# The down-projection of a two-layer trunk, done as seven block products, with sums made by negated copies and accumulating DMAs

## The chip, the core and the metric

One core of one Trainium2 chip runs the whole program. TensorE (PE in the profile) multiplies, VectorE (DVE), ScalarE (ACT) and GpSimd (POOL) do the rest, SyncE (SP) issues the DMAs. The metric is the device time of one execution in microseconds; three runs of the kernel before gave 2281.78, 2283.82 and 2288.46 us.

## The reference

Two layers run over 1024 prompt tokens and 64 sample tokens (8 sequences of 8), width 1024, inner width 2816, in float32. The change lies in the last matrix product of each layer and in the norm behind it:

```python
up = jnp.einsum('btd,df->btf', x, w_up)
hp = jnp.concatenate([conv_prefix, up], axis=1)
hc = conv_b + sum(conv_w[i] * hp[:, i:i + T] for i in range(CONV_WIDTH))
g, u = hc[..., :D_FF], hc[..., D_FF:]
y = jnp.einsum('btf,fd->btd', jax.nn.gelu(g, approximate=False) * u, w_down)
x = layer_norm(DEEPNORM_ALPHA * x + y, ln2_g, ln2_b)
```

The `x` of the last line is itself a norm's output, with gain `ln1_g` and bias `ln1_b`.

## The kernel before

The tokens are nine tiles: 0 to 7 of 128 prompt tokens, 8 (`NB`) with the 64 sample tokens. Every float32 operand is split into a rounded copy (`..h`, written by ACT) and the remainder (`..l`, a subtraction on DVE or POOL), and a product is three matmuls: high by high, high by low, low by high. The engines run programs of their own, with the order of work written out by hand and semaphores between them; nothing is reordered at run time.

A layer has four stages. The input projection and the mixing heads come first, then the output projection and a norm, whose result without gain and bias is kept in DRAM (`z_scr`). The up-projection then runs over 22 blocks `f` of 128 channels (gate and up); it is already computed as seven half-size products (`times`), with POOL making the sums of the weight blocks (`sum_up`, `lo_up`) and DVE joining the products (`joined`: `c11`, `u2`, `v`, ...). For each block ACT moves the sample columns (`moves`) and writes the first filter term (`tap_gate` into `hg[f % 2]`, `tap_up`), DVE adds the other terms (`conv_gate`, `conv_up`), ACT applies GELU, DVE multiplies (`product`), and SP stores the block to `a_scr[f]` (`act_rows`), 552 KB.

The down-projection goes over three groups of three tiles, and in each over all 22 rows `k` of blocks of `w_down`: a unit `d` loads `w_down[128k : 128k+128, :]` (512 KB) and the three tiles' columns of `a_scr[k]` (192 KB), ACT and DVE split both (`down_hi`, `act_hi`, `down_lo`, `act_lo`), and PE issues six matmuls of 512 columns a tile, four for the sample tile. Four slots hold split weights, three hold split activations, and a slot is written when PE has left the unit that used it. When a group ends, DVE adds the residual from PSUM (`joined_rz`), takes the statistics (`moments`), and later applies mean, deviation, gain and bias to the tile (`gained`, two instructions of 1024 columns). The residual itself is prepared by POOL: `residual` multiplies the tile read back from `z_scr` by the gain row and adds the bias row, two instructions a tile:

```python
pool.tensor_tensor(rz, rz, gain[0][0:tokens(t), :], ALU.mult).then_inc(S["xp1"], 1)
pool.wait_ge(S["xp1"], l * NTOK + t + 1)
pool.tensor_tensor(rz, rz, gain[1][0:tokens(t), :], ALU.add).then_inc(S["xp"], 1)
```

PE transposes finished tiles for the next layer (`turn_x`) between units, six tiles inside the down-projection and three behind it, and the input projection of layer 1 works on chunks of 384, 384 and 320 tokens (`two_chunks`). SP's queue carries all DMAs, in order; POOL issues none.

## Time and profile before

| | |
|---|---|
| runs | 2281.78, 2283.82, 2288.46 us, median 2283.82 |
| the profiled execution, its span | 2283.5 us |
| up-projection of layer 0, window | 580 to 877.3 us and before |
| down-projection of layer 0 | 877.3 to 1145.8 us |
| down-projection of layer 1 | ends at 2266.8 us |
| DMA, mean over the span | 118 GB/s |

The span runs from the first to the last instruction. The profile counts an engine as busy while it computes; PE and PEld (its weight loads) overlap. PEclk is the granted clock of TensorE as a share of full speed.

### The profile page before, as it was taken

What the parts mean: (1) busy time and instruction counts of PE and PEld (TensorE: products, weight loads), DVE (VectorE), ACT (ScalarE), POOL (GpSimd) and SP (SyncE); (2) the same over time, 40 slices, a digit from 0 to 9 for tenths busy, and PEclk for the clock granted to TensorE, in tenths of its full rate; (3) what the DMA queues carried; (4) which work ended last, traced back from release to release, by engine and by line L of the source; (5) the groups of instructions that cost most, each with busy time, mean ns of one, the idle gap of its engine ahead of it and who ended that gap; (6) DMA issues with size and microseconds to landing.
All of it is one profiled execution on the core that took longest, in us unless ns stands there. A gap on an engine that the chain in (4) does not pass through costs nothing.

```text
span 2283.5 us, 35524 instructions
## 1 busy us (share of the span) xinstructions
PE 2185.3 (96%) x14132; PEld 1986.4 (87%) x14132; DVE 1651.1 (72%) x2004; ACT 981.5 (43%) x1767; POOL 832.3 (36%) x444
## 2 busy tenths in 40 slices
PE   7999999899999999999999999989999999999996
PEld 7997677799999998888899876779999999988885
DVE  1477767878788886787636687677777878867677
ACT  3226755544344434343422276464434443443342
POOL 1115255554554450320311242446455445311311
PEclk9999999999999999999999999999999999999998
DMA  6303166223322325665562122641332233365762
GB/s 157 86 20 84 33 206 175 65 58 86 88 69 77 86 69 203 235 213 195 193 140 48 48 51 87 179 152 51 83 86 77 69 88 86 98 250 185 241 217 92
DMA packets 208766, 269.74 MB, mean 118 GB/s; under 512 B 31953, under 2 KB 167377, under 8 KB 208529
## 3 DMA queue, kind: packets, MB, share of 16 engines
q1 hardware_dynamic: 208600, 267.46, 39.2%
q8 instruction: 113, 1.85, 0.3%
q14 instruction: 53, 0.43, 0.1%
HBM read 217.65 MB, written 46.13 MB: 116 GB/s over the span
## 4 chain that ended last, share of the span: by engine, by line
PE 76%; DVE 14%; ACT 5%; issue 3%; POOL 2%; DMA 0%; SPq 0%; ACTq 0%; DVEq 0%; POOLq 0%
PE ps L2153 37%; PE ps L1872 17%; PE ps L1831 9%; PE ps L2092 5%; DVE bnst L1292 1%; PE ps L1897 1%; DVE rl L1491 1%; PE ps L1976 1%; DVE rzc L1278 1%; PE ps L1955 1%; DVE cb L1564 1%; POOL bl L762 1%; PE ps L1991 1%; DVE Sb L1610 1%; PE ps L2002 1%
## 5 line engine op out<-in xcount | busy, mean ns | idle before, releaser
L2153 PE MATMUL ps<-bt,bh 128*128 128x272 f32 (+1 forms) x3520 | 591.1, 290 | 18.7 <-DVE bt L1397 9.3
L2153 PEld LDWEIGHTS ps<-bt,bh 128*128 128x128 f32 x3520 | 503.3, 190 | 20.3 <-DVE bt L1397 9.7
L979 ACT ACTIVATE bh<-wblk 128x512 fp32r<-128x512 f32 x308 | 183.6, 624 | 483.1 <-POOL wblk L774 268.2
L2153 PE MATMUL ps<-bt,bl 128*128 128x272 f32 (+1 forms) x1760 | 369.1, 290 | 0.0
L2153 PEld LDWEIGHTS ps<-bt,bl 128*128 128x128 f32 x1760 | 278.4, 190 | 0.0
L762 POOL TENSOR_TENSOR bl<-wblk,bh 128x512 fp32r<-128x512 f32 x98 | 168.4, 1721 | 283.8 <-ACT bh L979 283.8
L1872 PE MATMUL ps<-rh,ah 128*128 128x512 f32 x792 | 245.6, 391 | 4.6 <-DVE ah L1502 3.2
L1872 PE MATMUL ps<-rl,ah 128*128 128x512 f32 x792 | 244.1, 389 | 0.0
L2153 PE MATMUL ps<-ba,bh 128*128 128x272 f32 (+2 forms) x1408 | 233.8, 288 | 4.0 <-DVE gu L1438 2.4
L1415 DVE TENSOR_TENSOR bl<-wblk,bh 128x512 fp32r<-128x512 f32 x210 | 169.0, 837 | 91.7 <-ACT bh L979 91.7
L1491 DVE TENSOR_TENSOR rl<-wrow,rh 128x1024 fp32r<-128x1024 f32 x132 | 189.5, 1437 | 42.5 <-ACT rh L1035 42.3
L1872 PE MATMUL ps<-rh,al 128*128 128x512 f32 x704 | 216.8, 389 | 0.0
L2153 PEld LDWEIGHTS ps<-ba,bh 128*128 128x128 f32 x1408 | 199.2, 188 | 5.3 <-DVE gu L1438 2.8
L787 POOL TENSOR_TENSOR rzd<-rzd,gain 128x1024 f32<-128x1024 f32 (+1 forms) x18 | 49.8, 2764 | 416.5 <-DMA rzd<-z_scr 416.5
L1831 PE MATMUL ps<-xh,wh 128*128 128x384 f32 (+1 forms) x576 | 194.1, 337 | 0.9 <-POOL wl L732 0.9
L1831 PE MATMUL ps<-xh,wl 128*128 128x384 f32 (+1 forms) x576 | 189.9, 330 | 0.0
L1831 PE MATMUL ps<-xl,wh 128*128 128x384 f32 (+1 forms) x576 | 189.7, 329 | 0.0
L740 POOL TENSOR_TENSOR rl<-wrow,rh 128x1024 fp32r<-128x1024 f32 x48 | 118.4, 2473 | 175.0 <-ACT rh L872 141.4
L1872 PEld LDWEIGHTS ps<-rh,ah 128*128 128x128 f32 x792 | 147.0, 188 | 38.3 <-issue 9.2
L1872 PEld LDWEIGHTS ps<-rl,ah 128*128 128x128 f32 x792 | 148.7, 188 | 31.1
L1035 ACT ACTIVATE rh<-wrow 128x1024 fp32r<-128x1024 f32 x132 | 138.1, 1049 | 45.1 <-DMA wrow<-in_w_down 30.8
L1872 PEld LDWEIGHTS ps<-rh,al 128*128 128x128 f32 x704 | 132.2, 188 | 27.7
(222 smaller groups left out, 4042.3 us busy)
## 6 DMA issues: line engine op xcount, KB each, us to landing
wrow<-in_w_down SPq DMA_DIRECT2D x132, 512.0 KB, 4.8
wblk<-in_w_up SPq DMA_DIRECT2D x88, 512.0 KB, 5.3
a_scr<-hg SPq DMA_DIRECT2D x44, 552.0 KB, 3.5
araw<-a_scr SPq DMA_DIRECT2D x88, 192.0 KB, 4.4
wrow<-in_w_out SPq DMA_DIRECT2D x48, 256.0 KB, 5.1
wrow<-in_w_out SPq DMA_DIRECT2D x24, 512.0 KB, 4.2
wraw<-in_w_in SPq DMA_DIRECT2D x10, 1024.0 KB, 6.3
z_scr<-rzc SPq DMA_DIRECT2D x16, 512.0 KB, 4.6
```

Source lines behind the costliest of these rows:

```text
L740: pool.tensor_tensor(rl[c % 2][:], wrow[(c + 2) % 4][:], rh[c % 2][:].bitcast(F32), ALU.subtract).then_inc(S["w_lo"], 1)
L762: pool.tensor_tensor(bl[b][:], block_of(f, b), bh[b][:].bitcast(F32), ALU.subtract).then_inc(S["u_lop"], 1)
L787: pool.tensor_tensor(rz, rz, gain[0][0:tokens(t), :], ALU.mult).then_inc(S["xp1"], 1)
L979: act.activation(bh[b][:], block_of(f, b), ACT.Copy).then_inc(S["u_hi"], 1)
L1035: act.activation(rh[dn_slot(d)][:], wrow[(d + 2) % 4][:], ACT.Copy).then_inc(S["d_hi"], 1)
L1278: e = dve.scalar_tensor_tensor(out=r, in0=r, scalar=ALPHA, in1=ps[0:q, 2 * i:2 * i + 2, :], op0=ALU.mult, op1=ALU.add)
L1415: dve.tensor_tensor(bl[b][:], block_of(f, b), bh[b][:].bitcast(F32), ALU.subtract).then_inc(S["u_lov"], 1)
L1491: dve.tensor_tensor(rl[s][:], wrow[(d + 2) % 4][:], rh[s][:].bitcast(F32), ALU.subtract).then_inc(S["d_lo"], 1)
L1831: e = nc.tensor.matmul(out, lhs, rhs, start=(m == 0), stop=(m == n - 1))
L1872: e = nc.tensor.matmul(ps[:, 2 * i + half, :], lhs, rhs[:, 512 * half:512 * half + 512], start=(first and m == 0), stop=(final and m == le ...
L2092: e = nc.tensor.matmul(ps[:, 2 * i + n, :], m_tile(t, KORD[kk], low), right[:, 512 * n:512 * n + 512], start=start, stop=stop)
L2153: e = nc.tensor.matmul(up_half(f, b, n), lhs, rhs[:, c:HW_] if n else rhs[:, 0:c], start=(k == 0 and m == 0), stop=(k == HK - 1 and m == 2))
```

## The change

Two things keep their form: the split into high and low parts, and 128x512 results in PSUM. The down-projection is now one level of a seven-product scheme. Prompt tokens are halved (tiles 0 to 3, tiles 4 to 7), the inner rows are halved (even and odd blocks `f`), and the output columns are halved (0 to 511, 512 to 1023). Each of the seven products (`P_1`, `P_2`, `P_3`, `P_6`, `P_5`, `P_7`, `P_4`, in this order) has 11 steps `s`, in which four token tiles of one operand block meet one 128x512 piece of a weight block. The sample tokens aren't part of the scheme; their rows ride along in the four products whose right side is a plain block of `w_down`.

The sums that the scheme needs are made in three ways. On the activations: ACT writes a negated copy of half a block (`negated`), SP stores it to the new DRAM buffers `e_scr` and `f_scr` (`neg_out`), and POOL issues accumulating DMAs that add other half blocks on top (`act_add`, three for each pair of blocks), while the up-projection runs. On the weights: the four blocks are loaded once a layer and stay in SBUF; ACT writes a negated copy of a block (`weight_neg`), and an accumulating DMA from `w_down` adds a block to it (`weight_add`), so `T_1`, ..., `T_4` come one after the other. On the results: the first product is copied to `p1`, DVE adds or subtracts products from PSUM into the residual rows `rzd` (`join`, `second`), and four accumulating DMAs add `p1` to the residual rows (`residual_add`).

All nine residual tiles are in SBUF at once. ACT multiplies the two rows of the first norm by ALPHA (`scaled_gains`), and POOL still multiplies and adds them. The gain and the bias row of the second norm are now applied by POOL for tiles 0 to 3, 8 and 5 (`gained`), behind a normalising instruction on ACT (`normal2`), and by DVE for tiles 4, 6 and 7. The input projection of layer 1 takes chunks of 512, 288 and 288 tokens, and five tiles are transposed inside the down-projection. The core of the diff:

```diff
-CH = [(0, 384), (384, 768), (768, T)]
+CHS = [[(0, 384), (384, 768), (768, T)]] + [[(0, HT), (HT, 800), (800, T)]] * (DEPTH - 1)
...
+KP = FT // 2
+NP = 7
+NST = NP * KP
+P_1, P_2, P_3, P_6, P_5, P_7, P_4 = range(NP)
+PX, PY, PZ = [6, 7, 2, 5], [3, 4, 0, 1], [2, 5, 6, 7]
+P_BANKS = {P_1: PX, P_2: PY, P_3: PX, P_6: PY, P_5: PX, P_7: PY, P_4: PZ}
+P_SAMP = {P_1: PY[3], P_2: PX[0], P_3: PY[0], P_5: PY[0]}
+BY_POOL = [0, 1, 2, 3, 8, 5]
+BY_DVE = [4, 6, 7]
+KGRP = [(0, 4), (4, 8), (8, KP)]
+X_AT = {62: 0, 64: 1, 68: 2, 70: 3, 72: 8}
...
+            def neg_out(l, k, which):
+                sp.wait_ge(S["neg"], neg_a(l, k, which) + 1)
+                if which == 0:
+                    sp.dma_start(e_scr[k, :, 0:3:2, :], hx[:, 0:1, :].to_broadcast([P, 2, HT])).then_inc(S["e_out"], 16)
+                else:
+                    sp.dma_start(f_scr[k], hx[:, 1, :]).then_inc(S["f_out"], 16)
...
+                sp.wait_ge(S["u_p"], 7 * (l + 1) * FT)
+                down_block(l, "w11", 2, 4, 7)
+                down_block(l, "w11", 3, 7, KP)
+                for s in range(4, NST):
+                    if s == 4:
+                        gains(l, 0)
+                        gains(l, 1)
+                        z_back(l, NB)
+                    elif s in (5, 7):
+                        z_back(l, s - 5)
+                        z_back(l, s - 4)
+                    elif s == 6:
+                        sample_raw(l, 2)
+                        down_block(l, "w21", 0, 0, 6)
+                    elif s == 8:
+                        down_block(l, "w21", 1, 6, KP)
+                    elif s == 9:
+                        act_rows(l, FT - 1)
...
+                    elif s == 17:
+                        down_block(l, "w22", 0, 0, KP)
+                    elif s == 18:
                         conv_rows(l, NRB - 1)
...
+                    act_block(l, s)
...
+            def act_add(l, k, i):
+                n = l * KP + k
+                if i == 0:
+                    pool.wait_ge(S["e_out"], 16 * (n + 1))
+                    pool.dma_start(e_scr[k, :, 0:3:2, :], hg[0][:, HT:2 * HT].unsqueeze(1).to_broadcast([P, 2, HT]),
+                                   accum_op=ALU.add).then_inc(S["adds0"], 16)
+                elif i == 1:
+                    pool.wait_ge(S["prod"], l * FT + 2 * k + 2)
+                    pool.wait_ge(S["a_out0"], 32 * (n + 1))
+                    pool.wait_ge(S["adds0"], 16 * (n + 1))
+                    pool.dma_start(e_scr[k, :, 1:3, :], hg[1][:, HT:2 * HT].unsqueeze(1).to_broadcast([P, 2, HT]),
+                                   accum_op=ALU.add).then_inc(S["adds1"], 16)
+                else:
+                    pool.wait_ge(S["f_out"], 16 * (n + 1))
+                    pool.wait_ge(S["adds1"], 16 * (n + 1))
+                    pool.dma_start(f_scr[k], e_scr[k, :, 2, :], accum_op=ALU.add).then_inc(S["adds2"], 16)
...
+            def weight_add(l, which, g):
+                k0, k1 = KGRP[g]
+                tile, block, c = {T_1: (w11, 0, HT), T_2: (w22, 1, HT), T_3: (w12, 0, HT), T_4: (w21, 1, 0)}[which]
+                pool.wait_ge(S["neg"], neg_t(l, which, g) + 1)
+                after(pool, f"wadd{g}", 16 * (4 * l + which))
+                src = w_down[l].rearrange("(k two p) n -> two p k n", two=2, p=P)[block][:, k0:k1, c:c + HT]
+                pool.dma_start(tile[:, k0:k1, :], src, accum_op=ALU.add).then_inc(S[f"wadd{g}"], 16)
...
+            def gained(l, t):
+                n, q = l * len(BY_POOL) + BY_POOL.index(t), tokens(t)
+                rz = rzd[t][0:q, :]
+                if t == 0:
+                    pool.wait_ge(S["gain_landed"], 64 * (l + 1))
+                pool.wait_ge(S["ln_z"], z2_n(l, t) + 1)
+                pool.tensor_tensor(rz, rz, gain[2][0:q, :], ALU.mult).then_inc(S["n_ym"], 1)
+                pool.wait_ge(S["n_ym"], n + 1)
+                pool.tensor_tensor(rz, rz, gain[3][0:q, :], ALU.add).then_inc(S["n_yp"], 1)
...
                 for f in range(1, FT):
                     lo_up(l, f, B_11)
                     lo_up(l, f, B_12)
-                    for b in SUMS:
+                    for b in SUMS[:3]:
                         sum_up(l, f, b)
+                    sum_up(l, f, B_S3)
+                    if f >= 5 and f % 2:
+                        act_add(l, (f - 5) // 2, 2)
+                    if f >= 3 and f % 2:
+                        act_add(l, (f - 3) // 2, 0)
+                    elif f >= 4:
+                        act_add(l, (f - 4) // 2, 1)
+                act_add(l, KP - 2, 1)
+                residual(l, NB)
+                act_add(l, KP - 2, 2)
+                act_add(l, KP - 1, 0)
+                weight_add(l, T_1, 0)
+                for t in range(4):
                     residual(l, t)
+                act_add(l, KP - 1, 1)
+                weight_add(l, T_1, 1)
+                act_add(l, KP - 1, 2)
+                weight_add(l, T_1, 2)
+                residual_add(l, R_P1)
+                for t in range(4, NB):
+                    residual(l, t)
+                for which in (T_2, T_3, T_4):
+                    for g in range(len(KGRP)):
+                        weight_add(l, which, g)
+                for which in (R_U2T, R_U2B, R_U2C):
+                    residual_add(l, which)
+                for t in TOP:
+                    gained(l, t)
...
                 if f >= 2:
-                    act.wait_ge(S[f"a_out{f % 2}"], 16 * (l * (FT // 2) + f // 2))
+                    if f % 2:
+                        act.wait_ge(S["a_out1"], 16 * (l * KP + f // 2))
+                        act.wait_ge(S["adds1"], 16 * (l * KP + f // 2))
+                    else:
+                        act.wait_ge(S["a_out0"], 32 * (l * KP + f // 2))
+                        act.wait_ge(S["adds0"], 16 * (l * KP + f // 2))
                 act.activation(hg[f % 2][:], gu[f % 2][:, 0, C0:C0 + CV], ACT.Identity, scale=par[:, f, 16:17], bias=par[:, f, 19:20])\
...
+            def negated(l, k, which):
+                act.wait_ge(S["prod"], l * FT + 2 * k + which + 1)
+                after(act, ("adds0", "f_out")[which], 16 * (l * KP + k))
+                act.activation(hx[:, which, :], hg[which][:, 0:HT], ACT.Copy, scale=-1.0).then_inc(S["neg"], 1)
...
+                for s in range(NST):
+                    if s + 2 < NST:
+                        down_hi(l, s + 2)
+                        act_hi(l, s + 2)
...
+                    elif 58 <= s < 63:
+                        if s < 62:
+                            deviation2(l, TOP[s - 58])
+                        if s == 61:
+                            deviation2(l, NB)
+                        normal2(l, TOP[s - 58])
...
+                for s in range(NST):
+                    if s + 2 < NST:
+                        down_lo(l, s + 2)
+                        act_lo(l, s + 2)
...
+                    elif s in (57, 58):
+                        for i in range(2):
+                            stats(l, 2 * (s - 57) + i, 1)
+                            moments2(l, 2 * (s - 57) + i)
+                        if s == 58:
+                            scaled2(l, 0)
+                    elif s == 59:
+                        stats(l, NB, 1)
+                        moments2(l, NB)
+                        scaled2(l, 1)
+                    elif s in (60, 61):
+                        scaled2(l, s - 58)
+                        for i in range(2):
+                            join(l, J_VB, 2 * (s - 60) + i)
...
+                    lh_, ll_, rh_, rl_ = ah[s % 3][:, P * i:P * i + P], al[s % 3][:, P * i:P * i + P], dh[s % 3][:], dl[s % 3][:]
+                    for m, (lhs, rhs) in enumerate(((lh_, rh_), (lh_, rl_), (ll_, rh_))):
+                        e = nc.tensor.matmul(ps[:, P_BANKS[p][i], :], lhs, rhs, start=(fresh and m == 0), stop=(final and m == 2))
...
+                for s in range(2, NST - 3):
+                    down_ready(s)
+                    down_step(s)
+                    if s == 4:
+                        rows_turn(NRB - 1)
+                    if l < DEPTH - 1 and s in X_AT:
+                        turn_x(l + 1, X_AT[s])
+                for tiles in ((0, 1), (2, 3)):
+                    for s in range(NST - 3, NST):
+                        down_ready(s)
+                        down_step(s, tiles)
```

## Rows read from the trace of the kernel before

**Rows 1.** the page, part 1: busy time, share of the span, instructions:

```profile
span 2283.5 us, 35524 instructions
...
PE 2185.3 (96%) x14132; PEld 1986.4 (87%) x14132; DVE 1651.1 (72%) x2004; ACT 981.5 (43%) x1767; POOL 832.3 (36%) x444
...
```

**Rows 2.** engine busy by window: layer 0, up-projection, then down-projection:

```profile
...
core 0: us, PE busy (x) PEld busy (x) DVE busy (x) ACT busy (x) POOL busy (x), PEclk, DMA share, GB/s
580.00:877.30 297.30, 297.30 (x2376) 297.30 (x2375) 237.70 (x258) 124.40 (x211) 137.83 (x79) 1.00 0.29 83
877.30:1145.80 268.50, 266.61 (x1197) 219.39 (x1196) 196.94 (x213) 109.01 (x173) 54.40 (x20) 1.00 0.62 208
...
```

**Rows 3.** timeline of PE, start of the down-projection of layer 0:

```profile
...
877.33 0.62 PE L1872 MATMUL ps<-rh,ah 128*128 128x512 f32 x2
...
889.14 0.39 PE L1872 MATMUL ps<-rh,al 128*128 128x512 f32 x1
```

**Rows 4.** groups by line and form, DVE: count, busy us, mean ns, idle before:

```profile
...
L1491 DVE TENSOR_TENSOR rl<-wrow,rh 128x1024 fp32r<-128x1024 f32 x132 | 189.5, 1437 | 42.5 <-ACT rh L1035 42.3
L1415 DVE TENSOR_TENSOR bl<-wblk,bh 128x512 fp32r<-128x512 f32 x210 | 169.0, 837 | 91.7 <-ACT bh L979 91.7
...
L1292 DVE BATCH_NORM_STATS2 bnst<-rzd 128x6 f32<-128x512 f32 x32 | 20.6, 685 | 0.4
...
```

**Rows 5.** timeline, both engines, while POOL prepares tiles 0 to 2:

```profile
...
917.84 1.23 DVE L1491 TENSOR_TENSOR rl<-wrow,rh 128x1024 fp32r<-128x1024 f32 x1 [1.24 <-ACT rh L1035]
...
921.67 3.42 DVE L1491 TENSOR_TENSOR rl<-wrow,rh 128x1024 fp32r<-128x1024 f32 x1
...
923.96 3.38 POOL L787 TENSOR_TENSOR rzd<-rzd,gain 128x1024 f32<-128x1024 f32 x1
...
925.01 2.75 DVE L1498 TENSOR_TENSOR al<-araw,ah 128x384 fp32r<-128x384 f32 x1
...
929.97 3.39 POOL L787 TENSOR_TENSOR rzd<-rzd,gain 128x1024 f32<-128x1024 f32 x1
...
```

**Rows 6.** ACT instructions by line, two answers: min/median/max ns, first and last start:

```profile
...
L905 ACT ACTIVATE rzc<-rzc,nmr,rst x18: 1231/1247/1252, 325.7 to 1525.5; 128x1024 f32<-128x1024 f32 x16, 64x1024 f32<-64x1024 f32 x2
...
L979 ACT ACTIVATE bh<-wblk x308: 612/620/638, 394.2 to 1982.6; 128x512 fp32r<-128x512 f32 x154
...
```

**Rows 7.** timeline of one block of the up-projection, all engines:

```profile
...
705.93 0.64 ACT L979 ACTIVATE bh<-wblk 128x512 fp32r<-128x512 f32 x1 [3.37 <-PE ps L2153]
...
707.83 1.28 POOL L781 TENSOR_TENSOR wblk<-wblk,wblk 128x512 f32<-128x512 f32 x1 [4.14 <-DVE bl L1415]
...
711.01 1.31 ACT L1011 ACTIVATE hg<-gu,par 128x1104 f32<-128x1104 f32 x1
...
719.68 0.71 DVE L1429 TENSOR_TENSOR gu<-gu,ps 128x544 f32<-128x544 f32 x1
...
728.47 1.28 POOL L781 TENSOR_TENSOR wblk<-wblk,wblk 128x512 f32<-128x512 f32 x1 [3.81 <-DVE bl L1415]
...
```

**Rows 8.** DMA issues: KB each, median us to landing:

```profile
...
a_scr<-hg SPq DMA_DIRECT2D x44, 552.0 KB, 3.5
...
gain<-in_ln_b SPq DMA_DIRECT2D x4, 512.0 KB, 8.9
...
```

**Rows 9.** one window of 5 us in the down-projection:

```profile
...
910.00:915.00 5.00, 5.00 (x24) 4.14 (x23) 2.39 (x4) 2.54 (x3) 0.00 (x0) 1.00 1.04 408
...
```

**Rows 10.** timeline of ACT and DVE around the start of the down-projection:

```profile
...
880.74 1.29 ACT L1018 ACTIVATE hu<-gu,par 128x1104 f32<-128x1104 f32 x1
...
884.58 1.36 DVE L1449 SCALAR_TENSOR_TENSOR hg<-gu,par,hg 128x1104 f32<-128x1104 f32 x1
...
```

**Rows 11.** timeline, end of the kernel:

```profile
...
2266.41 0.61 PE L1872 MATMUL ps<-rl,ah 128*128 128x512 f32 x2
...
2278.60 1.28 DVE L1316 SCALAR_TENSOR_TENSOR rzd<-rzd,rst,gain 64x1024 f32<-64x1024 f32 x1
```

**Rows 12.** waits of PE at the layer boundary (us, times, longest):

```profile
...
PE ps L1850 <- DVE xl L1259: 1.6, 1, 1.6
...
```

More of the change, by code:

```diff
@@ L364, in m_part, with half_of @@
+        def half_of(t, half):
+            return rzd[t][0:tokens(t), HT * half:HT * half + HT]
         def m_part(op, low):
@@ new lines, in scaled_gains, with first_out, deviation2 @@
+            def scaled_gains(l):
+                act.wait_ge(S["gain_landed"], 64 * l + 32)
+                for n in range(2):
+                    act.activation(gain[n][:], gain[n][:], ACT.Copy, scale=ALPHA).then_inc(S["gain_ok"], 1)
+            def first_out(l):
+                for i in range(4):
+                    act.wait_ge(S["d_tile"], 4 * (l * NP + P_1) + i + 1)
+                    act.activation(p1[:, i, :], ps[:, PX[i], :], ACT.Copy).then_inc(S["p1_ev"], 1)
+            def deviation2(l, t):
+                q = tokens(t)
+                act.wait_ge(S["ln_ag"], ln2_n(l, t) + 1)
+                act.activation(rst2[0:q, t, :], mv2[0:q, t, 1:2], ACT.Sqrt, bias=epsT[0:q, 0:1]).then_inc(S["ln_sd"], 1)
@@ L1073, in body @@
                 else:
-                    for t in G3[2]:
+                    for t in range(4, NB):
                         x_hi(l, t)
@@ new lines, in second, with stats @@
+            def second(l, i):
+                dve.wait_ge(S["d_tile"], 4 * (l * NP + P_6) + i + 1)
+                dve.wait_ge(S["radd"], 16 * (RADDS * l + R_P1))
+                dve.tensor_tensor(p1[:, i, :], p1[:, i, :], ps[:, PY[i], :], ALU.add).then_inc(S["joins"], 1)
+            def stats(l, t, half):
+                q = tokens(t)
+                if t == NB:
+                    dve.wait_ge(S["joins"], JOINS * l + (J_S5 if half else J_S2) + 2)
+                else:
+                    j = (J_VT if half else J_C11) if t < 4 else J_C22 if half else J_C21
+                    dve.wait_ge(S["joins"], JOINS * l + j + t % 4 + 1)
+                dve.bn_stats(out=bst[0:q, t, 6 * half:6 * half + 6], in_=half_of(t, half)).then_inc(S["ln_bn"], 1)
@@ new lines, in body @@
+                    if l < DEPTH - 1 and s in X_AT:
+                        x_lo(l + 1, X_AT[s])
+                for t in (4, 5):
+                    join(l, J_C21, t - 4)
+                    stats(l, t, 0)
+                    moments2(l, t)
+                scaled2(l, 4)
+                scaled2(l, 5)
+                dve.wait_ge(S["gain_landed"], 64 * (l + 1))
+                gained(l, 4)
+                for t in (6, 7):
+                    join(l, J_C21, t - 4)
+                    stats(l, t, 0)
+                    moments2(l, t)
@@ L1818, in body @@
+                scaled2(l, 6)
+                gained(l, 6)
+                scaled2(l, 7)
+                gained(l, 7)
                 if l < DEPTH - 1:
-                    for t in G3[2]:
+                    for t in range(4, NB):
                         x_lo(l + 1, t)
@@ L1864, in turn_z @@
                 for k in range(KD):
-                    e = pe.transpose(ps[:, z_bank(t) + k // 4, P * (k % 4):P * (k % 4) + q], rzc[slot_of(0, t)][0:q, P * k:P * k + P], ident[0:q, 0:q])
+                    e = pe.transpose(ps[:, z_bank(t) + k // 4, P * (k % 4):P * (k % 4) + q], rzc[slot_of(t)][0:q, P * k:P * k + P], ident[0:q, 0:q])
                 e.then_inc(S["z_tr"], 1)
-            def six(i, pairs, first, final):
-                for m, (lhs, rhs) in enumerate(pairs):
-                    for half in range(2):
-                        e = nc.tensor.matmul(ps[:, 2 * i + half, :], lhs, rhs[:, 512 * half:512 * half + 512],
-                                             start=(first and m == 0), stop=(final and m == len(pairs) - 1))
-                return e
             pe.wait_ge(S["id_landed"], 16)
@@ new lines, in down_step @@
+                def down_step(s, tiles=(0, 1, 2, 3)):
+                    p, k = divmod(s, KP)
+                    if p in P_SAMP and k == KP - 1:
+                        down_samples(s)
+                    for i in tiles:
+                        down_tile(s, i)
+                    if p in P_SAMP and k < KP - 1 and 3 in tiles:
+                        down_samples(s)
+                down_ready(0)
+                down_step(0, (0, 1))
+                down_ready(1)
+                down_step(1, (0, 1))
```

822 lines of the change are left out of this document (525 added, 297 removed), and 2 rows, old and new, of the table S.

## The prediction, made before the changed kernel ran

> **What bounds the kernel now.** I read the page's first part, then the windows, then timelines inside the windows. TensorE (PE) is busy 2185.3 of 2283.5 us [rows 1]. The two windows of layer 0 show it busy without a gap through the up-projection and 266.6 of 268.5 us through the down-projection, at a granted clock of 1.00, its upper level of 2.4 GHz [rows 2]. So in these stages the time is the number of matmuls by the time of each. In the down-projection 52 matmuls of 512 columns start between 877.33 and 889.14 us, 0.227 us each [rows 3]. The windows give DVE as busy 196.9 us of that window, ACT 109.0, POOL 54.4, the DMA engines 0.62 [rows 2]: there is room, if nothing has to wait in the wrong place.
>
> **What it removes.** Per layer the old down-projection issues 22 x (8 x 6 + 4) = 1144 matmuls. The new one issues 7 products x 11 steps x 4 tiles x 3 = 924, and 4 x 11 x 2 = 88 for the sample rows: 1012. The shape stays 128x128 by 512 columns. 132 fewer x 2 layers x 0.227 us = **-59.9 us**. A step is now 12 matmuls, 2.72 us, or 14, 3.18 us, where the sample rows ride along (first, second, third and fifth product). PE transposes the same nine tiles between layers. The input projection of layer 1 has the same matmuls over 512 + 288 + 288 instead of 384 + 384 + 320 columns, 1088 both ways: nothing.
>
> **Work per step, and lead.** A step needs two ACT copies of 128x512 at 0.62 us [rows 6] and two DVE subtractions of 128x512, 0.62 (half of the 1.23 us that 1024 columns take when POOL is idle [rows 5]) to 0.84 us, the mean with POOL beside them [rows 4]. That is 1.3 us on each engine against 2.72 us. The joins (42 a layer) and statistics (18) of 512 columns cost DVE about 0.7 us each [rows 4], 42 us in 225. All hidden by mean load. With three operand slots DVE ends step s about 1.9 us after PE ends step s-3, so PE has a lead of 2 x 3.18 - 1.9 = 4.4 us (3.5 us at 2.72): any delay beyond that is lost.
>
> **POOL beside DVE.** Here is the change's first price. While POOL multiplies and adds the residual's gain and bias rows, DVE and POOL take turns: POOL ran 3.38 and 3.39 us, DVE's two subtractions took 3.42 and 2.75 us, of which the first takes 1.23 alone and the second, with 384 columns, less, and two POOL instructions with two of DVE took 929.97 - 923.96 = 6.0 us [rows 5]. With the new 512-column pairs (0.6 + 0.6 instead of 1.23 and about 0.5) I take 5.5 us a pair. Before, a unit of 18 matmuls (4.1 us) needed such a pair and three such units passed under PE's lead; now a step of 3.18 us needs one. The Trainium skill ("SBUF — State Buffer", Who interferes with whom) says that a DVE instruction with two SBUF inputs contends with a GpSimd instruction that reads SBUF and that one waits out the other; the trace agrees, and by that rule the joins, which read PSUM, go free.
>
> *Residual rows.* Tiles 0 to 3, then 4 to 7: eight POOL instructions in a row each, four pairs, 22 us against 12.7 us of PE, 9.3 late, less the lead of 4.4: 5 us. Two stretches, two layers: **+20 us**. Lower bound 0 (if POOL's DMA waits space them out), upper 9.3 x 4 = 37.
>
> *Gain and bias rows after the norm*, moved from DVE (five tiles) to POOL, steps 58 to 62. Here ACT and DVE also go in lockstep: ACT issues the normalising instruction of a tile (1.25 us [rows 6]) only after DVE's `scaled2`, DVE does that after the subtractions of step s+2, and ACT's copies for s+3 are queued behind it. In a round, counted from the end of a normalising instruction: POOL starts its two instructions, ACT copies, DVE's two subtractions are done after 6.2 us, scalar work 0.35 (1.2 in the first, with statistics), ACT 1.25: 7.8 to 8.7 us. From the start of PE's step 58: first tile normalised at 5.3; operands of step 61 at 11.5, of 62 at 20.2, 63 at 28.0, 64 at 35.8, 65 at 41.0. Undisturbed, 65 would start at 7 x 2.72 = 19.0. So **+22 us a layer, +44**. Lower bound: POOL alone sets the pace, 27 us for ten instructions against 13.6, less the lead, 10 a layer; and 0 if DVE slips between.
>
> **Start of the stage.** Step 2's operands come after ACT's `tap_up`, which ended 4.7 us after the stage's start at 882.0 [rows 10], a new negation (0.62) and two copies (1.24): DVE at 884.5, PE wants it at 883.7. Then DVE's two gate instructions (2.75, two like the 884.58 row), GELU (1.2, a little under the 1.31 of `tap_gate` [rows 7]), the copies (1.24) and the last subtraction of step 3: 890.3, 2.6 late; then two more filter instructions and sample rows: 1.7 late. 5.1 us, less the old stage's own 0.9 in this place: **+8.5 us**. DMA: about 9.5 MB must land before step 8's operands, SP's queue being in order; at 408 GB/s [rows 9] that is 23 us against the 25 of eight steps, so I add nothing; at the 286 GB/s of the up-projection (83 / 0.29 [rows 2]) it would be 33, +8 a layer. The two later bursts (4.5 MB around step 17) stand behind four slots of prefetch.
>
> **Accumulating DMAs in the up-projection.** The trace of before has none, and no DMA from POOL. `tap_gate` of block f now waits for an addition out of the buffer it overwrites, and POOL issues that only after the last block sum of f+1. In the trace that sum ends at 709.1 and `tap_gate` starts at 711.0; what hangs on it (gate filter, `c11`, up filter, `u2`) ends at 720.4 [rows 7]. PE ended the product that reuses `u2`'s banks at 705.9 and so starts the next, 24 matmuls of 0.125 us [rows 2], at 705.9 + 20.6 - 3.0 = 723.5. Slack 3.1; the DMA may take 1.9 + 3.1 = 5.0 us, and each us more is a us per block. The plain store of the same buffer lands in 3.5 us [rows 8]; an accumulation reads its target too, 0.52 MB, 1.3 us at 408 GB/s; 0.3 for POOL: 5.1, the edge. In every second block another DMA stands ahead of it: 0.34 us to issue and 0.26 MB twice over, +1.0 to 1.6. I take +1.0 us in ten blocks a layer: **+20 us**. Bounds: 0 (3.5 us as the store), and 8.9, the slowest landing [rows 8]: 3.9 and 4.9 us, 84 a layer. The Trainium skill ("DMA: Bandwidth & Descriptors", Specifications) gives about 1 us to the first byte from GpSimd against about 0.6 from the hardware path; no run here shows it. By it the sum would be 0.1 us larger per block, some 4 us.
>
> The later accumulations (weights, 1 MB, needed five to seven steps on, 14 us or more; the residual, 9 steps on) would have to take three times a plain load to be felt: nothing.
>
> **Ends.** At the layer boundary tiles 4 to 6 must be split before the second chunk, and DVE splits them after its last gained tile, 11 us after the last matmul; the first chunk covers 10.9 us. I take +2 us on the old 1.6 [rows 12]: **+2**. End of the kernel: from the last matmul (2266.8) to DVE's last (2279.9) 13.1 us [rows 11], then 3.6 for the store. Now two half tiles remain at the last matmul: join, statistics, two gained tiles, 11.4 us: **-1.7**.
>
> **Sum.** -59.9 + 20 + 44 + 8.5 + 20 + 2 - 1.7 = +32.9. The profiled run is 2283.5 us, the median of the runs 2283.8, so they may be compared: 2283.5 + 32.9 = **2316 us**. By itself the down-projection comes out about even: 30 us less work a layer, 36 us of waits.
>
> **Rivals.**
> 1. *The shared port does not reach PE.* If DVE's instructions slip between POOL's, or the lockstep does not form, the 64 us go: 2252 us. For it: in the old stage PE lost 1.9 us in all beside the same overlap [rows 2, 5]. Against: step and lead are shorter. It decides from about half: with 40 of the 64 us gone the kernel is faster. Chance 0.26.
> 2. *The accumulations are slow.* At 6.7 us instead of 5.1, 1.7 and 2.7 us a block, 42 a layer, 33 more than the ten of the forecast: 2316 + 66 = 2382 us; at 8.9, 2464. For: the target is read and written in memory. Against: the DMA engines are 0.29 busy there [rows 2]. Chance 0.22.
> 3. *Bytes bound the start.* 8 us a layer more: 2332 us, within the forecast's own range. Chance 0.10.
> 4. Forecast: 0.42, own range 2295 to 2340.
>
> Less than 0.3% (7 us) I can't tell from no change. Faster: rival 1 and little more, 0.27. Same: the crossing between rival 1 and the forecast, 0.08. Slower 0.65. The range goes from 2242 (rival 1 with half of the 20 us of the DMAs gone) to 2400 (rival 2).
>
> **What would show it.** 1012 matmuls of 512 columns a layer at 0.227 us. DVE's `dl` and `al` subtractions with maxima near 3.3 us where POOL works on `rzd`; PE waiting for DVE `al` in steps 61 to 65 for about 5 us each. In the up-projection, idle time of ACT before L1011's successor released by a DMA, and blocks of alternating length, 20.7 and 21.7 us. The forecast is wrong if the window of the up-projection is unchanged, or longer by over 40 us, or if the 77 steps take less than 250 us.

## The result, and the profile after

The changed kernel takes 2564.6 us (median of 4 runs, 2562.4 to 2571.1) against 2283.2 us for the kernel before (4 runs): a ratio of 1.1227, 95% interval 1.1205 to 1.1248. It is 281 us slower, where 33 us were forecast; 2565 lies far outside the range of 2242 to 2400. The profiled run has a span of 2565.0 us.

Page of the changed kernel, parts 1, 3 and 4 (beside [rows 1]):

```profile
PE 2232.4 (87%) x13868; PEld 1997.6 (78%) x13868; DVE 1671.0 (65%) x2064; ACT 1044.6 (41%) x1867; POOL 994.7 (39%) x566
...
q1 hardware_dynamic: 222424, 261.69, 32.7%
q0 software_dynamic: 31008, 60.30, 14.7%
...
PE ps L2713 11%; DMA e_scr<-hg 10%; PE ps L2301 9%; DMA araw<-a_scr 4%; POOL wblk L969 3%; PE ps L2560 3%; POOL bl L961 3%; POOL wblk L973 3%; DVE al L1913 2%; POOL wblk L977 2%; DVE hg L1873 2%; DVE hg L1870 2%; POOL wblk L980 2%; DVE dl L
```

PE has fewer matmuls and yet is "busy" longer (2232 against 2185 us), and two DMAs stand in the chain that ended last: POOL's accumulation `e_scr<-hg` with 10%, the load `araw<-a_scr` with 4%. Windows of layer 0: the whole up-projection of the kernel before, then the up-projection and the down-projection of the changed kernel (the down-projection before is in [rows 2]):

```profile
396.40:877.30 480.90, 469.51 (x3726) 468.46 (x3727) 385.95 (x424) 207.83 (x350) 237.18 (x136) 0.99 0.28 79
```

```profile
399.30:984.10 584.80, 502.37 (x3726) 495.55 (x3727) 387.18 (x425) 215.91 (x370) 266.04 (x165) 0.93 0.42 106
984.10:1291.15 307.05, 257.44 (x1057) 205.73 (x1056) 199.48 (x245) 131.10 (x201) 101.85 (x50) 0.92 0.72 191
```

The up-projection, whose matmuls the change doesn't touch, grew by 103.9 us (480.9 to 584.8); the down-projection, with 11.5% fewer matmuls, by 38.5 (268.5 to 307.05). Layer 1 repeats it, with 578.8 and 305.2 us. Both windows also show a lower granted clock of TensorE, 0.93 and 0.92 instead of 0.99 and 1.00: PE stood idle again and again, and the same 3726 instructions of the up-projection count 502 us of busy time instead of 470. In the down-projection the matmuls are busy 257.4 us, where 266.6 less 30 would be 236.6: about 21 us of that stage went into slower matmuls, the rest of its loss into waiting. Waits of PE over the whole kernel (us in total, times, longest):

```profile
PE ps L2621 <- ACT gu L1276: 134.0, 40, 7.4
PE ps L2713 <- DVE al L1913: 96.5, 25, 9.3
```

**The up-projection.** Timeline of one even and the start of one odd block (start, us; in brackets the idle time before and what ended it):

```profile
718.54 1.29 POOL L980 TENSOR_TENSOR wblk<-wblk,wblk 128x512 f32<-128x512 f32 x1 [3.82 <-DVE bl L1836]
719.77 1.19 POOL L993 DMA_DIRECT2D e_scr<-hg  x1
...
725.56 1.31 ACT L1304 ACTIVATE hg<-gu,par 128x1104 f32<-128x1104 f32 x1 [3.87 <-DMA e_scr<-hg]
...
728.49 0.60 ACT L1276 ACTIVATE gu<-ps 128x544 f32<-128x544 f32 x1
729.15 0.77 PE L2621 MATMUL ps<-bt,bh 128*128 128x272 f32 x4 [1.58 <-ACT gu L1276]
...
743.19 1.29 POOL L980 TENSOR_TENSOR wblk<-wblk,wblk 128x512 f32<-128x512 f32 x1 [3.81 <-DVE bl L1836]
...
744.42 0.88 POOL L998 DMA_DIRECT2D f_scr<-e_scr  x1
...
745.01 1.55 POOL L987 DMA_DIRECT2D e_scr<-hg  x1
```

POOL ends its last block sum (L980) at 719.83 and issues the accumulation at once; `tap_gate` (L1304) starts only when that has landed, at 725.56, 5.7 us after the sum. In the odd block the smaller accumulation stands ahead in the queue, and `tap_gate` started at 753.13, 8.7 us after the sum. From L980 to L980 the block takes 24.65 us, the next one 28.2 (to 771.35); before, 20.6 [rows 7]. PE's wait is named after `snap` (L1276), which ACT does behind `tap_gate`, `tap_up` and the new negation. What hangs on `tap_gate` on DVE runs without a gap, up to the split (L1836) that POOL's next last sum waits for:

```profile
726.90 1.37 DVE L1870 SCALAR_TENSOR_TENSOR hg<-gu,par,hg 128x1104 f32<-128x1104 f32 x1 [5.08 <-ACT hg L1304]
...
735.79 2.43 DVE L1889 TENSOR_TENSOR hg<-hg,hu 128x1104 f32<-128x1104 f32 x1
...
738.15 2.38 DVE L1836 TENSOR_TENSOR bl<-wblk,bh 128x512 fp32r<-128x512 f32 x2
...
742.43 0.68 DVE L1836 TENSOR_TENSOR bl<-wblk,bh 128x512 fp32r<-128x512 f32 x1
```

Line L1304 by itself, over the whole kernel, what it waited for (us in total, times):

```profile
  DMA e_scr<-hg: 202.2, 38
```

202 us of waiting in 38 of 44 blocks: the two up-projections together grew by as much, 201.8 us.

**The down-projection.** Idle times of PE in its first 100 us, timeline of layer 0:

```profile
991.91 0.50 PE L2713 MATMUL ps<-dh,ah 128*128 128x512 f32 x1 [1.28 <-DVE al L1913]
997.60 0.50 PE L2713 MATMUL ps<-dh,ah 128*128 128x512 f32 x1 [2.22 <-DVE al L1913]
1005.22 0.50 PE L2713 MATMUL ps<-dh,ah 128*128 128x512 f32 x1 [2.52 <-DVE al L1913]
1026.32 0.80 PE L2713 MATMUL ps<-dh,ah 128*128 128x512 f32 x1 [9.35 <-DVE al L1913]
...
1039.79 0.79 PE L2713 MATMUL ps<-dh,ah 128*128 128x512 f32 x1 [4.43 <-DVE al L1913]
...
1066.51 0.79 PE L2713 MATMUL ps<-dh,ah 128*128 128x512 f32 x1 [8.06 <-DVE al L1913]
```

All wait for DVE's subtraction `al`, but for two reasons. Waits of ACT (first) and of DVE (second) in 984 to 1090:

```profile
ACT ah L1363 <- DMA araw<-a_scr: 43.0, 10, 10.5
...
DVE al L1913 <- ACT ah L1363: 28.1, 7, 10.4
```

ACT itself waits 43 us for the activations: `araw` loads stand in SP's queue behind weights and residual rows. And DVE, where POOL works at residual rows (timelines of DVE and of POOL):

```profile
1017.61 8.65 DVE L1913 TENSOR_TENSOR al<-araw,ah 128x512 fp32r<-128x512 f32 x1
1026.19 2.85 DVE L1909 TENSOR_TENSOR dl<-w,dh 128x512 fp32r<-128x512 f32 x1
1028.96 2.88 DVE L1913 TENSOR_TENSOR al<-araw,ah 128x512 fp32r<-128x512 f32 x1
...
1045.37 0.68 DVE L1909 TENSOR_TENSOR dl<-w,dh 128x512 fp32r<-128x512 f32 x1
```

```profile
1017.22 2.68 POOL L1008 TENSOR_TENSOR rzd<-rzd,gain 64x1024 f32<-64x1024 f32 x1
...
1021.96 3.75 POOL L1006 TENSOR_TENSOR rz_top<-rz_top,gain 128x1024 f32<-128x1024 f32 x1
1025.78 2.70 POOL L1008 TENSOR_TENSOR rz_top<-rz_top,gain 128x1024 f32<-128x1024 f32 x1
```

A subtraction takes 0.68 us alone, 2.85 beside POOL, and one 8.65. From about 1105 us the stage runs as forecast, PE busy 94.2 of 95 us, until POOL multiplies the rows after the norm: PE idles 3.08, 3.53, 2.03 and 4.32 us in rounds of 8.1, 7.4 and 7.4 us.

### The profile page after: what moved, and what is told of

It is laid out like the page before. It is cut to its first block, busy times and chain, and to the rows that moved or that the text cites. A ratio compares the mean times of both kernels' runs of the same rounds, so it can differ in the third digit from the quotient of the medians.

```text
span 2565.0 us, 35251 instructions
## 1 busy us (share of the span) xinstructions
PE 2232.4 (87%) x13868; PEld 1997.6 (78%) x13868; DVE 1671.0 (65%) x2064; ACT 1044.6 (41%) x1867; POOL 994.7 (39%) x566
## 4 chain that ended last, share of the span: by engine, by line
PE 33%; DVE 19%; POOL 15%; DMA 15%; issue 11%; ACT 8%; ACTq 0%; POOLq 0%; SPq 0%; DVEq 0%
PE ps L2713 11%; DMA e_scr<-hg 10%; PE ps L2301 9%; DMA araw<-a_scr 4%; POOL wblk L969 3%; PE ps L2560 3%; POOL bl L961 3%; POOL wblk L973 3%; DVE al L1913 2%; POOL wblk L977 2%; DVE hg L1873 2%; DVE hg L1870 2%; POOL wblk L980 2%; DVE dl L1909 2%; ACT hg L1304 2%
## 5 line engine op out<-in xcount | busy, mean ns | idle before, releaser
L2713 PE MATMUL ps<-dh,ah 128*128 128x512 f32 x616 | 260.8, 423 | 98.9 <-DVE al L1913 96.5
L2713 PE MATMUL ps<-dl,ah 128*128 128x512 f32 x616 | 254.4, 413 | 0.0
L2713 PE MATMUL ps<-dh,al 128*128 128x512 f32 x616 | 253.7, 412 | 0.0
L1909 DVE TENSOR_TENSOR dl<-w,dh 128x512 fp32r<-128x512 f32 x154 | 145.2, 943 | 151.1 <-ACT dh L1359 151.1
L1836 DVE TENSOR_TENSOR bl<-wblk,bh 128x512 fp32r<-128x512 f32 x210 | 167.9, 832 | 111.2 <-ACT bh L1267 111.0
L2713 PEld LDWEIGHTS ps<-dh,ah 128*128 128x128 f32 x616 | 124.6, 202 | 139.9 <-DVE al L1913 109.3
L1913 DVE TENSOR_TENSOR al<-araw,ah 128x512 fp32r<-128x512 f32 x154 | 164.2, 1066 | 62.7 <-ACT ah L1363 62.7
L2301 PE MATMUL ps<-xh,wh 128*128 128x288 f32 (+3 forms) x576 | 192.5, 334 | 1.1 <-POOL wl L931 1.1
L2301 PE MATMUL ps<-xl,wh 128*128 128x288 f32 (+3 forms) x576 | 188.6, 327 | 0.0
L2301 PE MATMUL ps<-xh,wl 128*128 128x288 f32 (+3 forms) x576 | 188.5, 327 | 0.0
L1359 ACT ACTIVATE dh<-w 128x512 fp32r<-128x512 f32 x154 | 96.4, 626 | 206.8 <-PE ps L2732 135.2
```

Source lines behind the costliest of these rows:

```text
L1359: act.activation(dh[s % 3][:], right_of(s), ACT.Copy).then_inc(S["d_hi"], 1)
L1836: dve.tensor_tensor(bl[b][:], block_of(f, b), bh[b][:].bitcast(F32), ALU.subtract).then_inc(S["u_lov"], 1)
L1909: dve.tensor_tensor(dl[s % 3][:], right_of(s), dh[s % 3][:].bitcast(F32), ALU.subtract).then_inc(S["d_lo"], 1)
L1913: dve.tensor_tensor(al[s % 3][:], araw[s % 4][:], ah[s % 3][:].bitcast(F32), ALU.subtract).then_inc(S["d_lo"], 1)
L2301: e = nc.tensor.matmul(out, lhs, rhs, start=(m == 0), stop=(m == n - 1))
L2713: e = nc.tensor.matmul(ps[:, P_BANKS[p][i], :], lhs, rhs, start=(fresh and m == 0), stop=(final and m == 2))
```

## The experiments

Working theory after this: (a) the accumulating DMAs stand inside a serial loop of the up-projection that has next to no slack; (b) POOL's row work holds up DVE; (c) the start of the down-projection waits for bytes. Twelve kernels follow, each against the kernel before on the same chip (2284 to 2285 us each time). e1 to e4 and e11 change the changed kernel, e6 to e9 build on e5, e10 on e9 and e12 on e10; e2, e3, e4, e11 and e12 leave out work and only measure.

**e1_adds_early.** In the up-projection loop of POOL:

```diff
-                    sum_up(l, f, B_S3)
                     if f >= 5 and f % 2:
                         act_add(l, (f - 5) // 2, 2)
...
+                    sum_up(l, f, B_S3)
```

> POOL issues the accumulating DMAs of a block before the block's last sum (it waits some 3.8 us there for DVE) instead of behind it; nothing else moves. Theory (serial loop): gate filter, joins, up filter, product, the splits of the next block, POOL's last sum, its DMA and ACT's tap_gate form one loop of about 19 us plus the landing, 5.7 us in one block and 8.7 in the next. Taking sum and wait (1.3 + 3.8 us, less 1.2 for the issue) out of it brings the even blocks back to 20.7 us and the odd ones to about 23: 4 us less in 19 blocks and 2 layers, about 2405 us. Rival (the accumulations take DMA or memory time that PE needs anyway, or the wait moves to another place): blocks stay at 24.7 and 27.6 us, within 20 us of 2565.

Measured: 2434.3 us (2428.3 to 2445.4; ratio 1.0669, 1.0631 to 1.0707). The up-projection takes 509.7 us; L1304 still waits 66.9 us. 130 us came back, the wait fell by 135. The theory holds; one line moved in POOL's order is worth 5% of the kernel. It gave 29 us less than hoped. The accumulation is now issued beside SP's stores and weight loads, and its median landing rose from 6.1 to 8.0 us; POOL's idle time ahead of its last sum also fell, from 3.8 to between 1.8 and 2.7 us, so the DMA leaves less early than I had counted. How much is due to each wasn't tested.

**e2_plain_copies.** `accum_op=ALU.add` left out of the three DMAs of `act_add`.

> The three DMAs that POOL issues per pair of blocks in the up-projection copy instead of accumulating, from the same place; so the sums are left out of e_scr and f_scr. Theory (it is the place in the loop that costs, the accumulation only some of the landing): the 512 KB DMA lands in 4.5 instead of 6.1 us (the plain store took 3.5), the 256 KB one a us earlier, so 1.5 to 2.5 us less per block, 60 to 95 us in all: 2470 to 2505 us. Rival (the accumulation is the cost): landing back to 3.5 us, nothing left to wait for, some 2360 us. Rival (the queue of POOL is the cost): no change.

Measured: 2445.6 us (one run); up-projection 524.9 us. Both sizes missed, below my band and above the rival's. DMA issues of the changed kernel and of this one (KB, us to landing):

```profile
e_scr<-hg POOLq DMA_DIRECT2D x44, 512.0 KB, 6.1
```

```profile
e_scr<-hg POOLq DMA_DIRECT2D x44, 512.0 KB, 3.6
...
e_scr<-hx SPq DMA_DIRECT2D x22, 512.0 KB, 2.7
```

So POOL's queue costs little: 3.6 us, where SP's store of as many bytes to the same buffer landed in 2.7. Accumulating costs 2.5 us. The landing is what the rival said, yet L1304 still waits 86.6 us (202.2 before the edit): 116 us less wait, 119 us less time. The place in the order (e1) and the accumulation (e2), each changed alone, take away over half of the wait.

**e3_one_column.** The operands of POOL's row instructions are cut, as `rz[:, 0:1]`, `gain[0][0:q, 0:1]`.

> POOL's multiplications and additions of gain and bias rows (residual rows and rows after the norm) are cut to one column, so that this work is left out; its DMAs and waits stay. Theory (the start of the down-projection is bound by DMA bytes, and the port costs only in the rounds of steps 58 to 62): the four long rounds shrink to the pace of PE, 13 us a layer, and the start gains at most 5 us a layer: 2530 to 2540 us. Rival (POOL and DVE at one port also cost the start): 35 to 40 us a layer more, about 2460 us.

Measured: 2493.2 us (one run), 71 us less; down-projections 276.8 and 270.8 us. Neither: twice what the theory allowed, and short of the rival. POOL's row work costs 36 us a layer, 30 and 34 of it in the down-projections; DVE's subtractions, 2.85 us beside it, are back at 0.69. But the stage is still no faster than before (268.5 us) with 132 matmuls fewer. In its first 108 us ACT waits for the activations as long as ever:

```profile
ACT ah L1363 <- DMA araw<-a_scr: 47.2, 13, 7.4
```

and the DMA engines' share is over 1 where PE idles:

```profile
1000.00:1015.00 15.00, 14.05 (x63) 11.22 (x62) 5.94 (x11) 8.98 (x13) 6.51 (x13) 1.00 1.07 345
1015.00:1030.00 15.00, 8.78 (x38) 6.62 (x36) 3.50 (x7) 5.26 (x9) 3.42 (x3) 0.90 1.11 259
1030.00:1045.00 15.00, 12.38 (x45) 10.08 (x46) 5.75 (x9) 5.35 (x9) 3.38 (x6) 0.76 1.08 300
1045.00:1060.00 15.00, 7.66 (x32) 5.35 (x30) 2.59 (x4) 2.30 (x4) 0.72 (x4) 1.00 1.06 330
```

The share alone doesn't decide it: in the first of these windows PE is busy 14 of 15 us at 1.07, and from 1105 to 1160 us 54.7 of 55 at 0.95. e6 and e10 below ask what the order of the loads is worth.

**e4_small_weight_adds.**

```diff
-                pool.dma_start(tile[:, k0:k1, :], src, accum_op=ALU.add).then_inc(S[f"wadd{g}"], 16)
+                pool.dma_start(tile[:, k0:k0 + 1, 0:16], src[:, 0:1, 0:16], accum_op=ALU.add).then_inc(S[f"wadd{g}"], 16)
```

> The twelve accumulating DMAs of weights a layer (11.5 MB) carry 16 columns of one block each instead of 1 MB, so the sums of weights are left out; order and waits stay. Theory (DMA bytes bound the start): 2.9 MB of accumulation lie in the first 103 us of the stage; at the 173 GB/s that POOL's queue reached there (5.5 MB in 30% of 106 us) that is 16 us a layer, and 30 us in all: about 2535 us. Rival (port, or order of the queue): within 6 us of 2565.

Measured: 2553.3 us (one run), 11 us less; both down-projections are some 7 us shorter (300.0 instead of 307.05). Between the two; with POOL's row work in place, taking the weights' accumulations away brings little.

**e5_adds_first.** As e1, but ahead of all sums, and the urgent one first:

```diff
                     lo_up(l, f, B_12)
+                    if f >= 3 and f % 2:
+                        act_add(l, (f - 3) // 2, 0)
+                    elif f >= 4:
+                        act_add(l, (f - 4) // 2, 1)
+                    if f >= 5 and f % 2:
+                        act_add(l, (f - 5) // 2, 2)
                     for b in SUMS[:3]:
```

> POOL issues the accumulating DMAs of a block right behind its two splits, before the block's sums, and that which tap_gate waits for first. In the run with them just before the last sum the up-projection still took 510 us (before: 481), and tap_gate waited 1.7 us for an accumulation in every even block. Theory (the place in POOL's order is all of it): the DMA starts some 7 us earlier, tap_gate waits for none, blocks are back at 20.7 us and the stage at 481 to 486: 2 x 26 less than 2434, about 2380 us. Rival (the issues, 0.9 to 1.6 us each, and the bytes cost by themselves): they now delay POOL's sums instead, and the stage stays within 8 us of 510: about 2425 us.

Measured: 2385.0 us (2382.2 to 2389.3; ratio 1.0444, 1.0425 to 1.0462). L1304 waits for no DMA. The up-projection:

```profile
398.40:887.70 489.30, 472.81 (x3727) 469.25 (x3728) 383.96 (x424) 215.46 (x370) 244.78 (x165) 0.99 0.49 126
```

As expected, but for 8 us that stay (489.3 against 480.9); they are there with all accumulations small too (e12), so they aren't the accumulations' bytes. PE waits 5 us more than before (17.4 against 12.3), mostly in ten places for one of DVE's joins (L1859, 6.2 us); why that join is late wasn't tested. Theory (a) is shown: by order alone 180 us of the 281 are gone, with the same DMAs and bytes.

**e6_spread, e7_spaced, e8_all.** In e6 SP's steps of the loads are changed (`w22` in `KGRP` at 17, 20, 23; `w12` at 28, 30, 32; `z_back` of tiles 4 to 7 at 25 and 33), and POOL does `residual(4)` to `residual(7)` between the `weight_add`s. In e7:

```diff
+N_AT = {58: 0, 60: 1, 63: 2, 65: 3, 67: 8}
...
-                        normal2(l, TOP[s - 58])
+                    if s in N_AT:
+                        normal2(l, N_AT[s])
```

and `scaled2` likewise. e8 is both.

> As e5_adds_first, and in the down-projection the load of 2.8 MB of w22 at step 17 is cut in three (steps 17, 20, 23), the 2.8 MB of w12 come at steps 28 to 32 instead of 12 to 21, the second half of z at steps 25 and 33 instead of 14 and 16, and POOL's residual work on it stands between the weight accumulations. Theory (bytes in one burst, with activations queued behind loads): with POOL's row work left out the first 100 us still lost some 40 us a layer; half of that or more comes back, 20 to 30 us a layer: about 2330 us. Rival (POOL's port sets the start): at most 6 us a layer, about 2370 us.

> As e5_adds_first, and the five tiles that POOL gives gain and bias after the norm are spaced over steps 58 to 67 (58, 60, 63, 65, 67) instead of 58 to 62. Theory (a pair of POOL instructions beside DVE's pair takes a round of 7.4 to 8.1 us; with two steps of PE for each, ACT's and DVE's operands keep their lead): the 13 us of idle PE in this stretch go, 26 us less than e5_adds_first. Rival (each pair costs DVE the same wherever it stands, and PE has no lead left): less than 8 us in all.

> All three changes together. If each is right and they add: 2380 - 50 - 26, about 2304 us. If the gains overlap (the residual work that was moved falls on steps that then have no lead): 2320 to 2350 us.

Measured: 2373.6 (ratio 1.0389, 1.0371 to 1.0406), 2392.5 (1.0475, 1.0459 to 1.0490) and 2387.2 us (1.0450, 1.0435 to 1.0466), where e5 has 2385.0. e6 brought 11 us, not 50. In its windows the start is better, but the steady part now loses 7 us where the residual rows went (e5 first, then e6):

```profile
1000.00:1110.00 110.00, 109.19 (x481) 89.88 (x480) 59.96 (x94) 55.94 (x81) 14.12 (x11) 1.00 0.82 187
```

```profile
1000.00:1110.00 110.00, 102.58 (x434) 83.00 (x432) 74.13 (x85) 51.30 (x73) 36.05 (x20) 0.97 0.90 207
```

e7 is 7 us slower instead of 26 faster, and e8 is no better than e5: my theory of the rounds was wrong in what it promised. With two or three steps between the normalisations PE still waits once for each of the five pairs of POOL: 3.09, 2.37 and 1.18 us, and then

```profile
1163.25 0.79 PE L2711 MATMUL ps<-dh,ah 128*128 128x512 f32 x1 [6.31 <-DVE al L1915]
...
1175.39 0.79 PE L2711 MATMUL ps<-dh,ah 128*128 128x512 f32 x1 [3.69 <-DVE al L1915]
```

That is 16.6 us, where e5 has four waits of 14.2 us in all. At both places where it was tried (e6, e7) the work on POOL kept its price.

**e9_rows_on_dve.** `residual` and `gained` of tiles 0 to 3 and 8 become DVE instructions; POOL keeps `gained(5)`:

```diff
+R_AT = {6: 8, 12: 0, 13: 1, 14: 2, 15: 3, 35: 4, 36: 5, 37: 6, 38: 7}
+G_AT = {60: 0, 61: 1, 62: 2, 63: 3, 64: 8}
...
+                    if s in R_AT:
+                        residual(l, R_AT[s])
+                    if s in G_AT:
+                        gained_rows(l, G_AT[s])
```

> As e5_adds_first, and the gain and bias rows of all residual tiles and of tiles 0 to 3 and 8 after the norm are multiplied and added by DVE (the same instructions, 1.23 us each alone) at steps 6, 12 to 15, 35 to 38 and 60 to 64; only tile 5 stays on POOL. Theory (while POOL works at rows, DVE's subtractions take 2.8 us instead of 0.68 and one took 8.65): with POOL's work cut to one column the down-projection took 274 us instead of 306; DVE now has 35 us of work more, of which some 6 us a layer aren't hidden: 281 us, 25 us a layer less than e5_adds_first, about 2335 us. Rival (DVE becomes the bound, rows in its order hold up operands as POOL did): 2375 us or more.

Measured: 2326.2 us (2325.9 to 2331.5; ratio 1.0187, 1.0168 to 1.0205), 59 us less than e5, where the theory had 50; down-projections 277.2 and 274.0 us. DVE is busy 182.7 us in the stage instead of 199.4, though it does more: no `al` subtraction of layer 0 takes over 0.69 us, so it no longer waits inside them. Not all of the 59 us need be that: in e5 POOL stood 48.5 us waiting for the gain rows with accumulations queued behind, and in e9 the first of these leaves 11 us ahead of the stage instead of 36 us into it. The clean measure of the row work is e3, which keeps waits and order.

**e10_rows_and_loads.** e9 with the loads spread, its residual rows of tiles 4 to 7 at steps 36, 38, 40, 42.

> As e9_rows_on_dve, with the loads of the down-projection spread: z of tiles 0 to 3 one at a time at steps 5, 7, 8, 10, the second part of w21 at 11 instead of 8, w22 in three parts at 16, 19, 22, z of tiles 4 to 7 at 24, 25, 33, 34, w12 at 28 to 32. Theory (what is left of the slow start is activations queued behind loads): 15 to 20 us a layer less than e9_rows_on_dve, about 2300 us. Rival (the accumulations alone hold the DMA engines): less than 5 us a layer, as e6_spread gained in all 11 us over e5_adds_first.

Measured: 2307.8 us (2305.5 to 2309.5; ratio 1.0100, 1.0084 to 1.0117), 18 us less than e9, where e6 brought 11: with the rows off POOL the loads' place counts for more, but for half of what I expected. This is the best version, still 1.0% slower than the kernel before.

**e11_gained_one_column.** Of e3's edit only the part in `gained`.

> The changed kernel with only the rows after the norm (tiles 0 to 3, 8 and 5) cut to one column on POOL; so this work is left out. Its residual rows stay whole. With both cut the kernel took 2493 us instead of 2565. Theory (PE idles 13 us a layer in steps 61 to 64): 26 us less than 2565, about 2538 us, and the residual rows are the other 46 us. Rival (the forecast's 22 us a layer): about 2520 us.

Measured: 2526.3 us (2519.2 to 2530.7; ratio 1.1056, 1.1026 to 1.1087): 38 us less, nearer to the forecast's 44 than to my 26 from the idle times, which leave out the lower clock (0.86) of that stretch. The residual rows are the other 33 (e11 to e3).

**e12_small_accumulations.** e10 with all accumulating DMAs cut to `0:16` of their last dimension, those of the weights to one block as well, as in e4.

> As e10_rows_and_loads, with every accumulating DMA (activations, weights, residual; 24 MB a layer by the page of the changed kernel's queue, 60.3 MB in all) cut to 16 columns of each row, so that these sums are left out; each is still issued and waited for. Theory (what is left of the loss at the start of the down-projection, some 20 us a layer, is the time that accumulations hold the DMA engines: windows with a share over 1 at 257 GB/s): the down-projection falls from 271 and 264 us to 250 to 255, the up-projection by 4 us or less, about 2270 us: only without their bytes the change would be faster than the kernel before. Rival (loads of weights and z bound the start by themselves): less than 6 us a layer, about 2298 us.

Measured: 2281.5 us (10 runs, 2277.4 to 2288.7; ratio 0.9986, 0.9975 to 0.9998), 26 us less than e10; up-projection unchanged (489.6), down-projections 257.9 and 254.3 us. Windows of that stage in e10 and in e12:

```profile
885.70:1157.20 271.50, 247.33 (x1054) 198.54 (x1054) 182.35 (x276) 130.28 (x201) 27.15 (x21) 0.96 0.80 215
```

```profile
891.30:1149.20 257.90, 241.80 (x1054) 195.78 (x1054) 181.78 (x275) 130.74 (x201) 22.67 (x21) 0.98 0.53 161
```

I had expected some 38 us, with 250 to 255 us for each down-projection, and the rival under 6 us a layer: the cause is shown, at two thirds of the size. So in the best order found the bytes of the accumulations cost 26 us. Without them the kernel is level with the one before, and the sums would still be owed: the two down-projections are 20 us shorter than before, not 60, and the up-projections 17 us longer.

## Why the prediction was wrong

The sign was right, the size off by 249 us; even without the ring of the up-projection (e5) the change is 100 us slower, three times the forecast. Term by term:

- **Matmuls, -59.9.** The count holds, and the steady part is busy 94.2 of 95 us. What it gives shows nowhere in the end, in part because the sum prices every matmul at 0.227 us: the stage had a granted clock of 0.92, and its matmuls took some 21 us longer than that price. This is contained in the terms for POOL and for the start below.
- **Accumulating DMAs in the up-projection, +20; about +180 by e5.** This is the step that failed: "Slack 3.1; the DMA may take 1.9 + 3.1 = 5.0 us". I looked for slack only up to `u2` and PE's product. DVE's program goes on: product, two splits, three joins, the split on which POOL's last sum waits; only behind that sum comes the next issue. That ring is closed, 24.65 - 5.7 = 19 us (28.2 - 8.7 = 19.5 in the odd block) plus the landing, so with a block of 20.6 us its slack was 1.7 us, the 1.9 that `tap_gate` already had. Every us beyond counts, and blocks of 24.65 and 28.2 us stand where I had 20.7 and 21.7. The landing itself was under-sized as well (5.7 for 5.1, and 8.7 for 6.1 to 6.7 with another DMA ahead). By itself, with the 5.0 us that I allowed, it would give 0.7 and 3.7 us a block, some 40 us a layer; the other 60 or so of the 103.9 are the false slack. Rival 2 named the mechanism, but its worst case of 84 a layer used the same false slack; and it was no cost of the accumulation alone, since e5 removes it without touching a byte.
- **POOL beside DVE, +20 and +44; 33 and 38 by e3 and e11.** The sum, 64, met 71, with some luck: one part was too small, the other too large. The lockstep came as described, with rounds of 7.4 to 8.1 us, but over four steps, not five, and the residual rows cost some eight us a stretch, not five. Rival 1 is refuted. What I didn't see: in e7 the lead doesn't absorb even a single pair.
- **Start of the stage, +8.5; some +75.** With POOL's row work out (e3) the stage took 276.8 and 270.8 us, where 268.5 and 263.8 less 30 plus 4 would be 242.8 and 238: 34 and 33 us a layer short. "I add nothing" failed: I compared the bytes needed by step 8 with the time of eight steps, at 408 GB/s. But loads for later steps stand in the same queue ahead of the activations, for which ACT waits 47.2 us in e3, and accumulations run beside them at about half the rate. e9 to e10 gives back 6 and 10 us of it by order, e10 to e12 another 14 and 10 by bytes. About 9 us of layer 0's 34 are the lower clock (PE busy 245.9 in e3, where 266.6 less 30 is 236.6); the rest wasn't taken apart. Rival 3 had the cause, with 8 us a layer a quarter of the size.
- **Boundary, +2, and tail, -1.7.** At the boundary PE waits 1.6 us for `xl` as before, and 2.2 for `xh`. From the last matmul (2550.0) to the end are 15.0 us against 16.7: right.
- **Not in the sum:** 8.4 us a layer by which the up-projection stays longer in e5. e12 rules out the accumulations' bytes; its cause stays open.

Together -60 + 180 + 71 + 75 + 17 is 283, against 281 measured. That it closes is no proof of the parts: 75 is what was left of the down-projections once POOL's rows were out.

## What to carry to other kernels

Before an operation is put into a pipelined loop, follow the ring from it back to itself, through each engine's program order and not only along the data, and subtract that length from the period: that is its slack. A busy share says nothing about it (DMA 0.29 here, and a DMA cost 8% of the kernel). An instruction that waits for an early event belongs ahead of those that wait for a late one in the same queue.

## What the runs showed of the hardware

**Accumulating DMAs hold the DMA engines longer.** In 600 to 950 us of the changed kernel POOL's queue moved 8.39 MB in 16.4% of the engines' time, 146 GB/s; as plain copies (e2, 600 to 900 us) 7.87 MB in 7.1%, 369 GB/s. That is 2.5 times the time per byte written. Over the down-projection it is 17.30 MB in 32.5% of 307 us, 173 GB/s, beside 41.1 MB in 39.5% of SP's queue, 339 GB/s.

**GpSimd's queue by itself is little slower.** In e2 a plain 512 KB copy from it landed in 3.6 us, SP's store of 512 KB to the same buffer in 2.7 us. The Trainium skill ("DMA: Bandwidth & Descriptors", Specifications) gives about 1 us to the first byte from GpSimd against about 0.6 on the hardware path; 0.9 us more here has the same sign and is larger.

**One DVE subtraction took 8.65 us** (0.68 alone), from within POOL's addition at 1017.22 to just after POOL's multiplication of the next tile, with three DMA issues of POOL between. It comes once a layer, at this place (8.66 us in layer 1), and e1, e5, e6, e7 and e11 have it too, with 8.65 to 8.67 us. The Trainium skill ("SBUF — State Buffer", Who interferes with whom) calls the port pair that DVE and GpSimd share an exclusive lock. The subtractions of 2.8 to 2.9 us beside POOL's instructions of 2.4 to 2.8 us agree with that; 8.65 us is longer than any one of POOL's (3.75 at most). With one column (e3) subtractions beside the same issues took 0.69 us, so the issues alone don't do it. Why this one lasted so long stays open.

**A starved PE is also a slower PE.** In the up-projection the same 3726 instructions were busy 502.4 us at a granted clock of 0.93, and 472.8 us at 0.99 in e5. Inside a ring that another engine sets this costs nothing by itself, but it hides idle time: PE's busy share fell only to 87%. In the down-projection, where PE sets the pace between its waits, it does cost: some 21 us of the stage's 307 at a granted clock of 0.92, by the numbers of the first section.
